# Encoder layer on eight cores: phase-boundary transfers cut into chunks

## The chip, the cores and the metric

The kernel is one program that runs on all 8 cores of one Trainium2 chip. The cores do not speak to each other: each computes 2,048 of the 16,384 tokens, with a halo of 128 tokens on both sides where neighbours are needed. The time is device microseconds of the slowest core. The profile is of one execution, on core 7, the slowest in it.

## What is computed

The reference is one layer of an encoder trunk, on x of 16384 x 2048:

```python
x = layer_norm(ALPHA * x + 0.5 * swiglu(x, ffn1...), ln1)
x = layer_norm(ALPHA * x + hybrid_mixer(x, ...), ln2)
x = layer_norm(ALPHA * x + 0.5 * swiglu(x, ffn2...), ln3)
# swiglu: (silu(x @ w_gate) * (x @ w_up)) @ w_down, with D_FF = 5632
# hybrid_mixer: h = x @ w_in, split into q | k | v | pool channels | gate_a | gate_b
#   y_a = banded attention(q, k, v) @ w_proj_attn        (16 heads, 4 kv heads, |t-s| <= 128)
#   y_b = multiscale pooling(pool channels) @ w_proj_pool
#   (sigmoid(gate_a) * y_a + sigmoid(gate_b) * y_b) @ w_out
```

## The kernel before

Activations are held feature-major: 16 chunks of 128 features on the partitions, tokens along the row. Everything large lies in one on-chip arena. Matmuls run in bf16; weights are f32 in DRAM and are cast by the transfer that loads them.

The work goes through phases, with a token tile each that fits the arena, and every intermediate is written to DRAM and read back by the next phase:

- Phase A, `ffn_phase` for the first SwiGLU, three tiles of 768 tokens: load x (`zf_load`, L420), cast to XB (L432), gate and up projections, down projection in two halves that accumulate into ZF. While the last half runs, `ln_stats` gathers sums. Then `ln_finish` normalizes ZF chunk by chunk: DVE subtracts and multiplies (L372, L380), ACT applies gain and bias in place (L384) and copies the chunk before to bf16 in XB (L387). After all 16 chunks, one store of ZF (L473), one of XB (L476), then the load of the next tile into ZF. `kvp_hook` follows on the same XB: key, value and pooling projections (K, V, P) with 8 weight pieces of `w_in`, and their stores (L510, L522, L534).
- Pooling (L541), two halves of 1,024 tokens.
- Attention (L623), two halves: 4 groups of heads (g) by 8 query blocks (i). The result AT is stored once at the end (L754), then the next stage's weights are prefetched.
- Merge (L771), two halves: projections and gates; MG is filled chunk by chunk (L810) and stored once (L812), then weights are prefetched.
- Output projection (L828), two halves: loads MG (L838) and the residual into ZF (L840), accumulates `w_out` into ZF (L851), `ln_stats`, `ln_finish`, then one store of ZF (L859) and one of the bf16 copy YB (L861), and prefetches.
- Phase C, `ffn_phase` again for the second SwiGLU, tiles of 768, 768 and 512 tokens. It has no bf16 output and no hook.

Order: each engine has its own instruction list, filled in program order. All activations' loads and stores are issued by SP, one after another. All weights are issued by POOL with `load_w` (L291), into a ring of 6 slots (8 in the merge phase), in order: a load waits until the matmuls that used its slot are done. `prefetch_w` issues loads ahead of a boundary. A `P.barrier()` stands at the end of each phase and of each half: every engine waits there for everything issued, all transfers included, prefetched weights too.

The waits are worked out from `Buf` objects. `_waits` adds, for each buffer read, its last write, and for each buffer written, its last write and all its reads:

```python
for b in reads:
    add(b.lastw)
for b in writes:
    add(b.lastw)
    for k, tok in b.reads.items():
        add(tok)
```

The destination in DRAM is such a buffer too: one for the whole of `x1T`, `x2T`, `attnTd`, `mrgTd` and `outT`. A wait on a transfer is put into the list of the engine that issues. In the output projection the four partial sums of `ln_stats` keep 4 of the 8 PSUM banks reserved.

Of the kernel before, what the change touches and what calls it, by code (L numbers as in the profile page):

```python
# [15 lines left out]
DC = 16  # L16
SEQ = 16384
TOWN = SEQ // NCORES
HALO = 128
# [12 lines left out]
C_LN = 0  # L32
# [141 lines left out]
def build_program():  # L174
# [16 lines left out]
    x1T = dt("x1T", [D, TPAD], F32, kind="Internal").ap()  # L191
# [5 lines left out]
    attnTd = dt("attnTd", [D, TOWN], BF16, kind="Internal").ap()  # L197
    mrgTd = dt("mrgTd", [D, TOWN], BF16, kind="Internal").ap()
    x2T = dt("x2T", [D, TOWN], F32, kind="Internal").ap()
    x2bT = dt("x2bT", [D, TOWN], BF16, kind="Internal").ap()  # L200

    def fm(ap2d, c0, nchunk, t0, nt):
        return ap2d[c0 * 128:(c0 + nchunk) * 128, t0:t0 + nt].rearrange("(c p) t -> p c t", p=128)

    ARENA_W = 51200
    with ExitStack() as stack:
# [8 lines left out]
        P = Prog(nc, stack)  # L215
# [87 lines left out]
        def acc(parts, rhs_fn, n_out, extra_reads, U):  # L303
# [3 lines left out]
            for (sa, sb, kc) in parts:  # L307
# [15 lines left out]
             reads=[cst_b], writes=[misc_b])  # L323
        pw_b = Buf("pw")
        P.dma("pool", lambda g: g.dma_start(out=pwsb[:], in_=pwg.rearrange("g (k p) n -> p g k n", p=128)),
              pw_b, writes=[pw_b])
# [24 lines left out]
                     t.matmul(o, onesS[:], r, start=f, stop=la),  # L351
                     reads=[qab, misc_b], writes=[qb[ui][1]], signal=True)

        def ln_finish(st, ZF, zf_b, Tt, units, lncol, YB, yb_b):
            sb, qb = st
            for ui, (u0, U) in enumerate(units):
                m = mean_sb[:, u0:u0 + U]
                r = rstd_sb[:, u0:u0 + U]
                P.op("act", lambda a, o=m, i=sb[ui][0][:, 0:U]: a.activation(o, i, AF.Copy),
                     reads=[sb[ui][1]], writes=[mean_b])  # L360
                P.op("dve", lambda v, o=r, i=m: v.tensor_tensor(o, i, i, ALU.mult),
                     reads=[mean_b], writes=[rstd_b])
                P.op("dve", lambda v, o=r, i=qb[ui][0][:, 0:U]:
                     v.scalar_tensor_tensor(o, i, EPS_P, o, ALU.add, ALU.subtract),
                     reads=[qb[ui][1], rstd_b], writes=[rstd_b])
                P.op("act", lambda a, o=r: a.activation(o, o, AF.Sqrt), reads=[rstd_b], writes=[rstd_b])
                P.op("dve", lambda v, o=r: v.reciprocal(o, o), reads=[rstd_b], writes=[rstd_b])  # L367
            for ap_, b_ in sb + qb:
                reserved.discard(banks.index(b_))
            def e_sub(c):  # L370
                z = ZF[:, c, :]
                P.op("dve", lambda v, z=z: v.tensor_tensor(z, z, mean_sb[:, 0:Tt], ALU.subtract),  # L372
                     reads=[zf_b[c], mean_b], writes=[zf_b[c]])

            e_sub(0)
            for c in range(DC):
                z = ZF[:, c, :]
                if c + 1 < DC:
                    e_sub(c + 1)
                P.op("dve", lambda v, z=z: v.tensor_tensor(z, z, rstd_sb[:, 0:Tt], ALU.mult),  # L380
                     reads=[zf_b[c], rstd_b], writes=[zf_b[c]])
                g = ccol(lncol + c)
                b = ccol(lncol + 16 + c)
                P.op("act", lambda a, z=z, g=g, b=b: a.activation(z, z, AF.Identity, bias=b, scale=g),  # L384
                     reads=[zf_b[c], cst_b], writes=[zf_b[c]])
                if YB is not None and c >= 1:
                    P.op("act", lambda a, o=YB[:, c - 1, :], z=ZF[:, c - 1, :]: a.activation(o, z, AF.Copy),  # L387
                         reads=[zf_b[c - 1]], writes=[yb_b])
            if YB is not None:
                P.op("act", lambda a, o=YB[:, DC - 1, :], z=ZF[:, DC - 1, :]: a.activation(o, z, AF.Copy),  # L390
                     reads=[zf_b[DC - 1]], writes=[yb_b])

        def ffn_phase(tiles, xf_d, xb_d, xb_cast, wg, wu, wd, lncol, outf_d, outb_d, hook):
# [7 lines left out]
            xb_b = Buf("xb")  # L401
            zf_ld = Buf("zfld")
            zf_b = [Buf("zf%d" % c) for c in range(DC)]
            ht_b = [Buf("ht%d" % c) for c in range(22)]
            st_b = Buf("zfst")
# [17 lines left out]
            for ti, (t0, units) in enumerate(tiles):  # L423
                Tt = sum(U for _, U in units)
                XB = xb_view(Tt)
                ZF = ZFf_[:, 0:DC * Tt].rearrange("p (c t) -> p c t", c=DC)
# [3 lines left out]
                if xb_cast:  # L430
                    for c in range(DC):
                        P.op("dve", lambda v, o_=XB[:, c, :], i_=ZF[:, c, :]: v.tensor_copy(o_, i_),  # L432
                             reads=[zf_b[c]], writes=[xb_b])
                elif ti == 0:
                    xb_load(0)
                for g in range(2):
                    for s in range(11):
# [3 lines left out]
                        for nn in range(2):  # L441
                            f = s * 2 + nn
                            for (u0, U) in units:
# [5 lines left out]
                                     reads=[bgb], writes=[tb])  # L449
# [3 lines left out]
                    if g == 1:  # L453
                        if (not xb_cast) and ti + 1 < len(tiles):
                            xb_load(ti + 1)
                        lnst = ln_begin(units)
                    for s in range(8):
# [11 lines left out]
                                ln_stats(lnst, ZF, zf_b, n - 2, Tt, units)  # L469
                ln_stats(lnst, ZF, zf_b, DC - 2, Tt, units)  # L470
                ln_stats(lnst, ZF, zf_b, DC - 1, Tt, units)
                ln_finish(lnst, ZF, zf_b, Tt, units, lncol, XB if outb_d is not None else None, xb_b)
                P.dma("sp", lambda s, i_=ZF, o_=fm(outf_d[0], 0, DC, outf_d[1] + t0, Tt):  # L473
                      s.dma_start(out=o_, in_=i_), st_b, reads=zf_b, writes=[outf_d[2]])
                if outb_d is not None:
                    P.dma("sp", lambda s, i_=XB, o_=fm(outb_d[0], 0, DC, t0, Tt): s.dma_start(out=o_, in_=i_),  # L476
                          xb_b, reads=[xb_b], writes=[outb_d[2]])
# [145 lines left out]
        for h in range(2):  # L623
# [24 lines left out]
                sxg_, o = carve(o, 512, F32)  # L648
                EGs.append((egf_, sxg_, Buf("eg%d" % i), Buf("sxg%d" % i)))
            assert o <= MAIN_W, (o, MAIN_W)  # L650
            x1_b, kt_b, vv_b, at_b = Buf("x1"), Buf("kt"), Buf("vv"), Buf("at")
            P.dma("sp", lambda s, o_=X1, i_=fm(x1bT, 0, DC, HALO + h * 1024, 1024): s.dma_start(out=o_, in_=i_),
                  x1_b, reads=[x1bT_db], writes=[x1_b])
            P.dma("sp", lambda s, o_=KT, i_=fm(kTd, 0, 4, h * 1024, 1280): s.dma_start(out=o_, in_=i_),
# [49 lines left out]
            def o_stage(g, i, pts):  # L704
                bO_ap, bO_b = next_bank()
                for j, (pa, pb, blk) in enumerate(pts):
                    P.op("pe", lambda t, o_=bO_ap, l=VV[:, blk, g * 128:(g + 1) * 128], r=pa, f=(j == 0), la=(j == 2):
                         t.matmul(o_, l, r, start=f, stop=la),  # L708
                         reads=[vv_b, pb], writes=[bO_b], signal=(j == 2))
                bD_ap, bD_b = next_bank()  # L710
                for j, (pa, pb, blk) in enumerate(pts):
                    P.op("pe", lambda t, o_=bD_ap, r=pa, f=(j == 0), la=(j == 2):
                         t.matmul(o_, ones1[:], r, start=f, stop=la),
                         reads=[misc_b, pb], writes=[bD_b], signal=(j == 2))
                dn, dnb = DNs[i % 2]
                P.op("dve", lambda v, o_=dn, i0=bD_ap, i1=EGs[g % 2][1]: v.tensor_tensor(o_, i0, i1, ALU.add),
                     reads=[bD_b, EGs[g % 2][3]], writes=[dnb])
                P.op("act", lambda a, o_=dn: a.activation(o_, o_, AF.Ln), reads=[dnb], writes=[dnb])
                P.op("act", lambda a, o_=dn: a.activation(o_, o_, AF.Exp, scale=-1.0), reads=[dnb], writes=[dnb])
                P.op("dve", lambda v, o_=AT[:, g * 4:(g + 1) * 4, i * 128:(i + 1) * 128],  # L720
                     i0=bO_ap.rearrange("p (h q) -> p h q", h=4), i1=dn.rearrange("p (h q) -> p h q", h=4):
                     v.tensor_tensor(o_, i0, i1, ALU.mult),
                     reads=[bO_b, dnb], writes=[at_b])

            def eg_build(g):
                egf_, sxg_, eg_b, sxg_b = EGs[g % 2]
# [15 lines left out]
            for si, (g, i) in enumerate(seq):  # L742
# [8 lines left out]
                if g < 3 and i < 4:  # L751
                    qpiece(g + 1, 2 * i)
                    qpiece(g + 1, 2 * i + 1)
            P.dma("sp", lambda s, i_=AT, o_=fm(attnTd, 0, DC, h * 1024, 1024): s.dma_start(out=o_, in_=i_),  # L754
                  at_b, reads=[at_b], writes=[attn_db])
            if h == 0:
                for g_ in range(3):
                    for s_ in range(2):
# [12 lines left out]
        for h in range(2):  # L771
# [7 lines left out]
            MGf, o = carve(o, DC * 1024, BF16)  # L779
            MG = MGf.rearrange("p (c t) -> p c t", c=DC)  # L780
            assert o <= MAIN_W
            at_b, mt_b, x1_b, mg_b = Buf("at"), Buf("mt"), Buf("x1"), Buf("mg")
            P.dma("sp", lambda s, o_=AT, i_=fm(attnTd, 0, DC, h * 1024, 1024): s.dma_start(out=o_, in_=i_),
                  at_b, reads=[attn_db], writes=[at_b])
            P.dma("sp", lambda s, o_=MT, i_=fm(mixTd, 0, 8, h * 1024, 1024): s.dma_start(out=o_, in_=i_),
# [3 lines left out]
            for s in range(8):  # L789
# [4 lines left out]
                for nn in range(2):  # L794
                    n = s * 2 + nn
                    for u in range(2):
# [11 lines left out]
                        P.op("dve", lambda v, o_=sb2, i0=byb: v.tensor_tensor(o_, i0, o_, ALU.mult),  # L808
                             reads=[bybb, sbb], writes=[sbb])
                        P.op("dve", lambda v, o_=MG[:, n, us], a_=sa, b_=sb2: v.tensor_tensor(o_, a_, b_, ALU.add),  # L810
                             reads=[sab, sbb], writes=[mg_b])
            P.dma("sp", lambda s_, i_=MG, o_=fm(mrgTd, 0, DC, h * 1024, 1024): s_.dma_start(out=o_, in_=i_),  # L812
                  mg_b, reads=[mg_b], writes=[mrg_db])
            if h == 0:
                for s_ in range(2):
                    prefetch_w(wpa, 0, 16, s_ * 256)
# [8 lines left out]

        x2T_db, x2bT_db = Buf("x2T"), Buf("x2bT")
        ring[0] = slots
        for h in range(2):  # L828
            o = 0
            MGf, o = carve(o, DC * 1024, BF16)  # L830
# [1 line left out]
            ZFf, o = carve(o, DC * 1024, F32)  # L832
            ZF = ZFf.rearrange("p (c t) -> p c t", c=DC)
            assert o <= MAIN_W
            mg_b, zf_ld = Buf("mg"), Buf("zfld")
            YB, yb_b = MG, mg_b
            zf_b = [Buf("zf%d" % c) for c in range(DC)]
            P.dma("sp", lambda s, o_=MG, i_=fm(mrgTd, 0, DC, h * 1024, 1024): s.dma_start(out=o_, in_=i_),  # L838
                  mg_b, reads=[mrg_db], writes=[mg_b])
            P.dma("sp", lambda s, o_=ZF, i_=fm(x1T, 0, DC, HALO + h * 1024, 1024): s.dma_start(out=o_, in_=i_),  # L840
                  zf_ld, reads=[x1T_db], writes=zf_b)
            units = [(0, 512), (512, 512)]
            lnst = ln_begin(units)
            for s in range(8):
                sl = load_w(wout, 0, 16, s * 256)
                for nn in range(2):
# [7 lines left out]
                        ln_stats(lnst, ZF, zf_b, n - 2, 1024, units)  # L854
            ln_stats(lnst, ZF, zf_b, DC - 2, 1024, units)
            ln_stats(lnst, ZF, zf_b, DC - 1, 1024, units)
            ln_finish(lnst, ZF, zf_b, 1024, units, C_LN + 32, YB, yb_b)
            st_b = Buf("zfst")
            P.dma("sp", lambda s, i_=ZF, o_=fm(x2T, 0, DC, h * 1024, 1024): s.dma_start(out=o_, in_=i_),  # L859
                  st_b, reads=zf_b, writes=[x2T_db])  # L860
            P.dma("sp", lambda s, i_=YB, o_=fm(x2bT, 0, DC, h * 1024, 1024): s.dma_start(out=o_, in_=i_),  # L861
                  yb_b, reads=[yb_b], writes=[x2bT_db])
            if h == 0:
# [105 lines left out]
```

How the kernel before makes its waits and increments, by code:

```python
    def replay(self, engname, handle):  # L164
        for waits, fn, inc in self.engs[engname].ops:
            for sem, val in waits:
                handle.wait_ge(sem, val)
            if fn is not None:
                ins = fn(handle)
                if inc is not None:
                    ins.then_inc(inc[0], inc[1])
```

## Time and profile before

| | us |
|---|---|
| median of 2 runs | 7022.39 (7019.82 to 7024.96) |
| the profiled execution | 7022.11 |
| its span (core 7, slowest) | 7020.6 |
| spans of the 8 cores | 6940.3 to 7020.6 |
| PE busy | 5719.6 |
| granted PE clock, mean | 0.910 |

Times in the rows are microseconds from the span's start. The profiled execution is 1.5 us longer than its span. "SPq" marks transfers issued by SP, "L300 POOL" those of weights. The time "to landing" runs from the issue to the completion semaphore.

### The profile page before, as it was taken

The page shows a single profiled execution, that of the slowest core. Times are in us where ns is not written, and L with a number is a line of the kernel's source. Part 1 is how long each engine was busy: PE and PEld are TensorE (multiplying, and loading weights), DVE is VectorE, ACT ScalarE, POOL GpSimd, SP SyncE. Part 2 cuts the span into 40 slices and gives each one's busy share as a digit, 9 for nine tenths or more (in the row PEclk, how much of TensorE's full clock was granted, in tenths as well). Part 3 has the DMA queues.
Part 4 walks back from the last instruction along what each step waited for, and adds up shares of the span by engine and source line. Part 5 has one row for each costly group of instructions (what it writes and reads, how often), then busy time and mean ns, then how long its engine had stood idle before and what let it go on. Part 6 is the DMA issues. An engine that isn't in the chain of part 4 may idle for free.

```text
span 7020.6 us, 83583 instructions; the slowest of 8 cores (6940.3 to 7020.6 us)
## 1 busy us (share of the span) xinstructions
PE 5719.6 (81%) x33856; PEld 3331.1 (47%) x33856; DVE 1212.6 (17%) x1834; ACT 1106.5 (16%) x1785; POOL 880.8 (13%) x729
## 2 busy tenths in 40 slices
PE   7999689996899961656479699537399989998997
PEld 4565455654556540212134244213256556565886
DVE  1111211112111124121211011032111131113112
ACT  0001200012000121343400001132100120002002
POOL 1111001110011103232300000000011111111111
PEclk9999899998999985878789799768699999999998
DMA  9898998989778774232366755744678788868998
GB/s 137 94 110 90 160 116 93 111 90 162 113 91 109 90 132 98 58 50 61 55 113 73 137 63 63 150 123 86 164 94 112 104 138 125 108 91 126 164 142 112
DMA packets 1142409, 756.63 MB, mean 108 GB/s; under 512 B 10128, under 2 KB 1070224, under 8 KB 1142032
## 3 DMA queue, kind: packets, MB, share of 16 engines
q0 software_dynamic: 1050640, 533.24, 65.1%
q1 hardware_dynamic: 91392, 218.03, 10.1%
q8 instruction: 277, 4.54, 0.3%
q14 instruction: 100, 0.82, 0.0%
HBM read 1179.05 MB, written 105.38 MB: 183 GB/s over the span
## 4 chain that ended last, share of the span: by engine, by line
PE 75%; DMA 9%; DVE 5%; another core or an unknown queue 4%; issue 3%; ACT 3%; POOL 1%; SPq 0%; ACTq 0%; DVEq 0%; POOLq 0%
PE ps L314 72%; DMA arena<-ffn_w_up 2%; DVE arena L372 2%; DMA arena<-x1bT 1%; DMA arena<-w_in 1%; DMA x2bT<-arena 1%; ACT arena L694 1%; PE ps L518 1%; DMA arena<-ffn_w_down 1%; DMA arena<-mrgTd 1%; DMA arena<-x2bT 1%; DVE arena L367 1%; DMA arena<-w_out 1%; ACT arena L732 1%
## 5 line engine op out<-in xcount | busy, mean ns | idle before, releaser
L314 PE MATMUL ps<-arena 128*128 128x384 bf16 (+2 forms) x32128 | 5391.4, 331 | 1026.5 <-DMA arena<-x1bT 191.5
L314 PEld LDWEIGHTS ps<-arena 128*128 128x128 bf16 x32128 | 3159.3, 98 | 3240.5 <-issue 1122.3
L448 ACT ACTIVATE arena<-ps 128x384 f32<-128x384 f32 (+1 forms) x528 | 249.5, 474 | 2977.8 <-PE ps L314 2977.8
L451 DVE TENSOR_TENSOR arena<-ps,arena 128x384 bf16<-128x384 f32 (+1 forms) x528 | 282.7, 536 | 2402.4 <-PE ps L314 2386.7
L300 POOL DMA_DIRECT2D arena<-ffn_w_gate x132 | 150.8, 1142 | 2209.6 <-PE ps L314 1961.0
L466 DVE SCALAR_TENSOR_TENSOR arena<-ps,arena 128x384 f32<-128x384 f32 (+1 forms) x384 | 205.7, 536 | 1171.8 <-PE ps L314 925.7
L300 POOL DMA_DIRECT2D arena<-ffn_w_down x192 | 203.2, 1061 | 1372.9 <-PE ps L314 1072.9
L341 ACT ACTIVATE arena<-arena 128x768 bf16<-128x768 f32 (+2 forms) x128 | 111.4, 871 | 942.6 <-DVE arena L466 549.3
L699 POOL TENSOR_TENSOR arena<-arena 128x512 bf16<-128x512 f32 x128 | 188.2, 1491 | 490.5 <-ACT arena L694 404.4
L300 POOL DMA_DIRECT2D arena<-ffn_w_up x132 | 151.4, 1147 | 280.1 <-PE ps L314 232.6
L806 DVE TENSOR_TENSOR arena<-ps,arena 128x512 f32<-128x512 f32 x64 | 44.3, 692 | 646.9 <-ACT arena L804 646.9
L384 ACT ACTIVATE arena<-arena,cstsb 128x768 f32<-128x768 f32 (+2 forms) x128 | 134.8, 1055 | 75.4 <-DVE arena L380 73.2
L708 PE MATMUL ps<-arena 128*128 128x512 bf16 x192 | 65.6, 413 | 95.2 <-POOL arena L699 95.2
L300 POOL DMA_DIRECT2D arena<-w_in x72 | 82.5, 1153 | 384.0 <-PE ps L314 263.7
L804 ACT ACTIVATE arena<-ps 128x512 f32<-128x512 f32 x64 | 38.3, 598 | 583.8 <-PE ps L314 583.8
L699 DVE TENSOR_TENSOR arena<-arena 128x512 bf16<-128x512 f32 x64 | 48.6, 759 | 461.2 <-ACT arena L694 461.2
L380 DVE TENSOR_TENSOR arena<-arena 128x768 f32<-128x768 f32 (+2 forms) x128 | 126.0, 990 | 0.0
L372 DVE TENSOR_TENSOR arena<-arena 128x768 f32<-128x768 f32 (+2 forms) x128 | 125.4, 985 | 0.0
L609 PE MATMUL ps<-arena,pwsb 128*128 128x512 bf16 x64 | 29.6, 617 | 112.1 <-DVE arena L601 112.1
L694 ACT ACTIVATE arena<-ps,cstsb 128x512 f32<-128x512 f32 x192 | 117.3, 684 | 1.7 <-POOL arena L699 1.7
L343 ACT ACTIVATE arena<-arena 128x768 bf16<-128x768 f32 (+2 forms) x128 | 109.3, 854 | 0.0
L851 DVE SCALAR_TENSOR_TENSOR arena<-ps,arena 128x512 f32<-128x512 f32 x64 | 44.1, 692 | 376.0 <-DMA arena<-x1T 195.9
(59 smaller groups left out, 1377.3 us busy)
## 6 DMA issues: line engine op xcount, KB each, us to landing
arena<-ffn_w_gate POOLq DMA_DIRECT2D x132, 1024.0 KB, 12.8
arena<-ffn_w_up POOLq DMA_DIRECT2D x132, 1024.0 KB, 17.1
arena<-ffn_w_down POOLq DMA_DIRECT2D x192, 704.0 KB, 11.5
arena<-w_in POOLq DMA_DIRECT2D x72, 1024.0 KB, 27.0
arena<-xT SPq DMA_DIRECT2D x3, 6144.0 KB, 56.2
x1T<-arena SPq DMA_DIRECT2D x3, 6144.0 KB, 24.8
arena<-x1bT SPq DMA_DIRECT2D x4, 4096.0 KB, 22.8
arena<-w_proj_attn POOLq DMA_DIRECT2D x16, 1024.0 KB, 15.1
```

What stands on the lines that cost most here:

```text
L300: P.dma("pool", lambda g, dst=dst, src=src: g.dma_start(out=dst, in_=src), b, writes=[b])
L314: t.matmul(o, l, r, start=f, stop=la),
L341: P.op("act", lambda a, o=za[:, 0:Tt], i=ZF[:, c, :]: a.activation(o, i, AF.Copy), reads=[zf_b[c]], writes=[zab])
L343: P.op("act", lambda a, o=qa[:, 0:Tt], i=ZF[:, c, :]: a.activation(o, i, AF.Square), reads=[zf_b[c]], writes=[qab])
L372: P.op("dve", lambda v, z=z: v.tensor_tensor(z, z, mean_sb[:, 0:Tt], ALU.subtract), reads=[zf_b[c], mean_b], writes=[zf_b[c]])
L380: P.op("dve", lambda v, z=z: v.tensor_tensor(z, z, rstd_sb[:, 0:Tt], ALU.mult), reads=[zf_b[c], rstd_b], writes=[zf_b[c]])
L384: P.op("act", lambda a, z=z, g=g, b=b: a.activation(z, z, AF.Identity, bias=b, scale=g), reads=[zf_b[c], cst_b], writes=[zf_b[c]])
L448: P.op("act", lambda a, o_=ta[:, 0:U], i_=bg: a.activation(o_, i_, AF.Silu), reads=[bgb], writes=[tb])
L451: v.tensor_tensor(o_, i0, i1, ALU.mult),
L466: v.scalar_tensor_tensor(z, i0, C_FFN, z, ALU.mult, ALU.add),
L694: a.activation(o_, i_, AF.Exp, bias=km, scale=SCALE),
L699: g_.tensor_tensor(o_, i0, i1, ALU.mult),
```

## The change

One large transfer becomes several at seven places. Stores that had to wait for a whole tile are issued for each part as soon as it is final:

- `ln_finish` gets a callback after L384's activation of chunk c; both `ffn_phase` and the output projection use it to store chunk c of ZF (384 KB for 768 tokens, 512 KB for 1,024, 256 KB for 512).
- AT is stored for each group of heads (4 stores of 1 MB), MG for each chunk (16 stores of 256 KB), inside their loops.
- The load of ZF in the output projection is issued as 4 loads of 4 chunks, each with a semaphore of its own.

The number of bytes and the rows of a transfer stay as they are. The destinations in DRAM keep their one buffer each.

```diff
+                if on_chunk is not None:
+                    on_chunk(c)
...
-                ln_finish(lnst, ZF, zf_b, Tt, units, lncol, XB if outb_d is not None else None, xb_b)
-                P.dma("sp", lambda s, i_=ZF, o_=fm(outf_d[0], 0, DC, outf_d[1] + t0, Tt):
-                      s.dma_start(out=o_, in_=i_), st_b, reads=zf_b, writes=[outf_d[2]])
+                def store_chunk(c, ZF=ZF, t0=t0, Tt=Tt):
+                    P.dma("sp", lambda s, i_=ZF[:, c, :],
+                          o_=outf_d[0][c * 128:(c + 1) * 128, outf_d[1] + t0:outf_d[1] + t0 + Tt]:
+                          s.dma_start(out=o_, in_=i_), st_b, reads=[zf_b[c]], writes=[outf_d[2]])
+
+                ln_finish(lnst, ZF, zf_b, Tt, units, lncol, XB if outb_d is not None else None, xb_b,
+                          on_chunk=store_chunk)
...
-                     reads=[bO_b, dnb], writes=[at_b])
+                     reads=[bO_b, dnb], writes=[at_g[g]])
+                if i == 7:
+                    P.dma("sp", lambda s_, i_=AT[:, g * 4:(g + 1) * 4, :], o_=fm(attnTd, g * 4, 4, h * 1024, 1024):
+                          s_.dma_start(out=o_, in_=i_), atst_b, reads=[at_g[g]], writes=[attn_db])
...
-                             reads=[sab, sbb], writes=[mg_b])
-            P.dma("sp", lambda s_, i_=MG, o_=fm(mrgTd, 0, DC, h * 1024, 1024): s_.dma_start(out=o_, in_=i_),
-                  mg_b, reads=[mg_b], writes=[mrg_db])
+                             reads=[sab, sbb], writes=[mg_c[n]])
+                    P.dma("sp", lambda s_, i_=MG[:, n, :], o_=mrgTd[n * 128:(n + 1) * 128, h * 1024:(h + 1) * 1024]:
+                          s_.dma_start(out=o_, in_=i_), mgst_b, reads=[mg_c[n]], writes=[mrg_db])
...
-            P.dma("sp", lambda s, o_=ZF, i_=fm(x1T, 0, DC, HALO + h * 1024, 1024): s.dma_start(out=o_, in_=i_),
-                  zf_ld, reads=[x1T_db], writes=zf_b)
+            for q4 in range(4):
+                P.dma("sp", lambda s, o_=ZF[:, q4 * 4:(q4 + 1) * 4, :], i_=fm(x1T, q4 * 4, 4, HALO + h * 1024, 1024):
+                      s.dma_start(out=o_, in_=i_), zf_ld4[q4], reads=[x1T_db], writes=zf_b[q4 * 4:(q4 + 1) * 4])
...
-            ln_finish(lnst, ZF, zf_b, 1024, units, C_LN + 32, YB, yb_b)
             st_b = Buf("zfst")
-            P.dma("sp", lambda s, i_=ZF, o_=fm(x2T, 0, DC, h * 1024, 1024): s.dma_start(out=o_, in_=i_),
-                  st_b, reads=zf_b, writes=[x2T_db])
+
+            def store_chunk4(c, ZF=ZF, h=h, zf_b=zf_b, st_b=st_b):
+                P.dma("sp", lambda s, i_=ZF[:, c, :], o_=x2T[c * 128:(c + 1) * 128, h * 1024:(h + 1) * 1024]:
+                      s.dma_start(out=o_, in_=i_), st_b, reads=[zf_b[c]], writes=[x2T_db])
+
+            ln_finish(lnst, ZF, zf_b, 1024, units, C_LN + 32, YB, yb_b, on_chunk=store_chunk4)
```

## Rows read from the trace of the kernel before

**Rows 1.** The page, part 1: busy time of the engines.

```profile
PE 5719.6 (81%) x33856; PEld 3331.1 (47%) x33856; DVE 1212.6 (17%) x1834; ACT 1106.5 (16%) x1785; POOL 880.8 (13%) x729
```

**Rows 2.** Chain of waits, whole span, in time: start, length, what.

```profile
835.19 31.20 PE ps L314 x192
...
1733.30 28.94 another core or an unknown queue
...
3106.49 66.38 another core or an unknown queue
...
3951.08 41.52 DMA arena<-w_in
...
4414.04 39.02 DMA arena<-w_out
4453.43 22.78 DMA arena<-mrgTd
...
4678.81 35.23 DMA x2bT<-arena
```

**Rows 3.** Timeline, end of phase A's first tile: start, length, what.

```profile
762.40 1.03 ACT L384 ACTIVATE arena<-arena,cstsb 128x768 f32<-128x768 f32 x1 [5.29 <-DVE arena L380]
...
813.38 2.62 SPq L420 DMA_DIRECT2D arena<-xT  x1
...
888.74 13.33 PE L314 MATMUL ps<-arena 128*128 128x384 bf16 x64 [22.35 <-DMA arena<-w_in]
...
902.18 10.96 DVE L432 CAST arena<-arena 128x768 bf16<-128x768 f32 x16 [66.39 <-PE ps L314]
```

**Rows 4.** Transfers issued from 730 to 930: number, KB, us to landing.

```profile
x1T<-arena SPq DMA_DIRECT2D x1, 6144.0 KB, 23.8
arena<-xT SPq DMA_DIRECT2D x1, 6144.0 KB, 56.2
```

**Rows 5.** Timeline, end of the second tile; landing of L420's loads.

```profile
1629.23 1.03 ACT L384 ACTIVATE arena<-arena,cstsb 128x768 f32<-128x768 f32 x1 [5.29 <-DVE arena L380]
...
1681.18 2.74 SPq L420 DMA_DIRECT2D arena<-xT  x1
...
DMA to landing us min/median/max: 27.6/33.8/62.3
```

**Rows 6.** A lone 3 MB store: in the chain, and in windows (DMA share, GB/s last).

```profile
2618.27 10.39 DMA pTd<-arena
...
2619.00:2620.00 1.00, 0.00 (x0) 0.00 (x0) 0.00 (x0) 0.00 (x0) 0.00 (x0) 1.00 0.85 338
...
2627.00:2628.00 1.00, 0.00 (x0) 0.00 (x0) 0.00 (x0) 0.00 (x0) 0.00 (x0) 0.50 0.33 111
```

**Rows 7.** Window in the attention boundary (DMA share and GB/s last).

```profile
3140.00:3150.00 10.00, 0.00 (x0) 0.00 (x0) 0.00 (x0) 0.00 (x0) 0.00 (x0) 0.50 1.08 106
```

**Rows 8.** Output projection: start of both halves, and the load of x1T.

```profile
4476.35 16.66 PE L314 MATMUL ps<-arena 128*128 128x512 bf16 x64 [65.22 <-DMA arena<-mrgTd]
...
4511.40 9.30 PE L314 MATMUL ps<-arena 128*128 128x512 bf16 x32 [18.39 <-DVE arena L851]
...
4773.97 9.42 PE L314 MATMUL ps<-arena 128*128 128x512 bf16 x32 [20.77 <-DVE arena L851]
...
arena<-x1T SPq DMA_DIRECT2D x1, 8192.0 KB, 56.6
```

**Rows 9.** Timeline, output projection, first chunk finished by L384.

```profile
4641.52 1.24 ACT L384 ACTIVATE arena<-arena,cstsb 128x1024 f32<-128x1024 f32 x1 [6.89 <-DVE arena L380]
```

**Rows 10.** Waits of PE between 6440 and 6960: us, times, longest.

```profile
PE ps L314 <- DMA arena<-ffn_w_down: 14.8, 6, 7.3
```

**Rows 11.** End of the kernel: timeline (L384, L474), and the store's landing.

```profile
6988.75 0.82 ACT L384 ACTIVATE arena<-arena,cstsb 128x512 f32<-128x512 f32 x1 [3.69 <-DVE arena L380]
...
7007.20 0.38 SPq L474 DMA_DIRECT2D outT<-arena  x1
...
outT<-arena SPq DMA_DIRECT2D x1, 4096.0 KB, 12.4
```

More of the change, by code:

```diff
@@ L352, in ln_stats, with ln_finish @@
                      reads=[qab, misc_b], writes=[qb[ui][1]], signal=True)
-        def ln_finish(st, ZF, zf_b, Tt, units, lncol, YB, yb_b):
+        def ln_finish(st, ZF, zf_b, Tt, units, lncol, YB, yb_b, on_chunk=None):
             sb, qb = st
@@ L650, in build_program @@
             assert o <= MAIN_W, (o, MAIN_W)
-            x1_b, kt_b, vv_b, at_b = Buf("x1"), Buf("kt"), Buf("vv"), Buf("at")
+            x1_b, kt_b, vv_b = Buf("x1"), Buf("kt"), Buf("vv")
+            at_g = [Buf("at%d" % g_) for g_ in range(4)]
+            atst_b = Buf("atst")
             P.dma("sp", lambda s, o_=X1, i_=fm(x1bT, 0, DC, HALO + h * 1024, 1024): s.dma_start(out=o_, in_=i_),
@@ L753, in build_program @@
                     qpiece(g + 1, 2 * i + 1)
-            P.dma("sp", lambda s, i_=AT, o_=fm(attnTd, 0, DC, h * 1024, 1024): s.dma_start(out=o_, in_=i_),
-                  at_b, reads=[at_b], writes=[attn_db])
             if h == 0:
@@ L781, in build_program @@
             assert o <= MAIN_W
-            at_b, mt_b, x1_b, mg_b = Buf("at"), Buf("mt"), Buf("x1"), Buf("mg")
+            at_b, mt_b, x1_b = Buf("at"), Buf("mt"), Buf("x1")
+            mg_c = [Buf("mg%d" % c) for c in range(DC)]
+            mgst_b = Buf("mgst")
             P.dma("sp", lambda s, o_=AT, i_=fm(attnTd, 0, DC, h * 1024, 1024): s.dma_start(out=o_, in_=i_),
@@ L827, in build_program @@
         ring[0] = slots
+        zf_ld4 = [Buf("zfld%d" % i) for i in range(4)]
         for h in range(2):
@@ L834, in build_program @@
             assert o <= MAIN_W
-            mg_b, zf_ld = Buf("mg"), Buf("zfld")
+            mg_b = Buf("mg")
             YB, yb_b = MG, mg_b
```

## The prediction

> **What bounds the kernel now.** PE is busy 5719.6 us of 7020.6 [rows 1]; the change touches none of its instructions. What can move is the rest, some 1300 us of idle PE. I read the chain of waits in order of time next: between long runs of L314 it passes through a few boundaries where nothing but transfers runs. The reader is to see there which transfer ends last [rows 2]: a piece of `w_in` at the end of phase A's tiles (shown as an unknown queue, 28.94 us at 1733, and 22.35 us at 888 [rows 3]), prefetched weights after attention and merge, and L861's bf16 store (35.23 us, and the same again in the second half) in the output projection. Then the timelines around each boundary, and last the transfers' own landing times.
>
> **The catch in the change.** Chunk stores name the same DRAM buffer as written. A written buffer adds a wait for its last write, and that is now the store of chunk c-1. So SP issues chunk c only when chunk c-1 has landed: the 16 stores of a tile form a chain, and each pays its whole latency. What a lone transfer pays: the 3 MB store issued at 2618.27 starts to move bytes at about 2619.15 (share 0.85 of that microsecond), stops near 2627.4 and lands at 2628.66 [rows 6]. So 3.15 MB took 8.25 us, 380 GB/s, and 10.39 - 8.25 = 2.1 us are fixed. The last store of the kernel, 4.19 MB in 12.4 us [rows 11], leaves 1.4 at that rate. I take 1.8, and 0.1 for SP to wake and issue. A chunk then takes 1.9 + 1.03 us at 384 KB, 1.9 + 1.38 at 512 KB, 1.9 + 0.69 at 256 KB: 3.0, 3.3, 2.6. L384 makes a chunk ready every 1.74 us in a tile of 768 (first at 763.4, all by 789.6, where the store that lands at 813.4 after 23.8 us was issued [rows 3, 4]), about 2.3 us for 1,024 tokens [rows 2, 9] and 1.2 us for 512 [rows 11]. So in `ln_finish` the store chain, not ACT, sets the pace. Bounds for 384 KB are 2.5 us from below (1.4 us fixed) and 5 us from above for 384 KB, since a contended megabyte costs more: 6 MB took 23.8 us with few weights beside it, while 9 MB (L476's 3 MB and xT's 6) took 56.2 us with them [rows 4], 1.6 times as long for each.
>
> The Trainium skill (DMA: Bandwidth & Descriptors, Anatomy of one DMA) speaks against cutting transfers that wait on each other: a fixed 2.0 us for each, mostly the receipt of the last write, plus bytes at 436 GB/s. By it the chunks take 2.9, 3.2 and 2.6 us, and the sum below would come out 3 to 6 us lower. It is fitted for the other issue path, and no chained small store is in this trace.
>
> **Phase A, tiles 0 and 1.** Chunk 0 is ready at 763.4 [rows 3]. Of the 16 chunks some run beside weights at about 4 us, others alone at 3.0; I take a mean of 3.6. They land by 763.4 + 57.6 = 821.0. Before, the one store landed at 813.4, where L420 is issued [rows 3]. So L476's store and the xT load, which have the SP queue behind it, run 7.6 us later: xT lands at 813.4 + 56.2 + 7.6 = 877.2. But the big store no longer stands in front of the `w_in` pieces between 789 and 813; the last piece, which landed at 888.7 behind more than 15 MB of the SP queue's, now meets less of it in its way and has until 835.19 + 31.20 = 866.4. I take its wait of 22.35 us as gone. P's last 64 matmuls then take 10.4 us instead of 13.33 (192 took 31.20 at full clock [rows 2]), so the cast L432 could start at 902.2 - 22.35 - 2.9 = 876.9. What is late next is xT itself, 877.2: gain 25.0 us. Tile 1: chunk 0 at 1630.3, chain ends 1687.9, 6.7 us after 1681.2; xT lands at 1681.2 + 62.3 + 6.7 = 1750.2 [rows 5]. P would end at 1733.3 + 10.4 = 1743.7; before, the cast began at about 1733.3 + 28.94 + 0.2 + 13.4 = 1775.9. Gain 25.7. Together 50; bounds 57 (xT never late) and 6 (chunks of 5 us: xT lands 22 us later still in both). L476's store and the K, V, P stores move later behind the chain on SP; only L451 of the next tile waits for them and PE has 8 free banks to run ahead. Tile 2 has no next load and no such wait: 0.
>
> **Attention, two halves.** 3 of AT's 4 MB leave the boundary; 3 stores run inside the loop, where no other transfer does. The boundary is bound by transfers together: 6 or 7 weight pieces and the store. 4 MB at 390 GB/s is 10.75 us of engine time, three quarters 8: gain 16 for both. Bounds: 0 if the weights set it alone, 26 if the store slows them by more than its own time. Merge: 15 of 16 chunks of MG leave: 10 us each, 20 for both, on 41.52 and 39.02 us [rows 2]; bounds 0 and 30. A chunk of MG is 112 matmuls of 512 columns, 24 us (384 columns took 31.20 / 192 = 0.1625 us each), so the chain of waits costs nothing there.
>
> **Load of ZF in quarters, two halves.** PE fills its 4 free banks in 16.66 us from 4476.35, then waits 18.39 us for L851, which needs x1T, all of it landing at 4453.8 + 56.6 = 4510.4 [rows 8]. MG landed first, at 4476.2 [rows 2], so the queue serves in order; the 8 MB then take 34.2 us, a quarter 8.6: it lands near 4485, before PE needs a bank at 4493. The later quarters land at 4493, 4502 and 4510, chunks 4, 8 and 12 are due at 4508 and every 31 us after. So 18.4 us go, and the 32 matmuls after it take 6.9 instead of 9.30 us since PE no longer falls to the low clock: 20.8. Second half: 20.77 + 2.5 = 23.3. Take 43; bounds 0 (quarters share the engines and land together) and 46.
>
> **Output projection, stores.** Chunk 0 ready at 4642.8 [rows 9], chunk 15 issued 15 x 3.3 later at 4692.3, its bytes out at 4694.5; L861's store, behind it on SP, needs 10.75 + 0.8 alone: lands near 4706, before 4714.0 (4678.81 + 35.23 [rows 2]). 8 us each, 16 for both. Bounds: 45 (no chain, store issued at 4678.8 lands at 4691.6) and -35 (chunks of 5 us).
>
> **Phase C.** Tile 0 to 1: the store was behind nothing PE waits for: 0; L420's load is issued later but is due only at the first down projection. Tile 1 to 2: the third tile is short of weights, PE waits 14.8 us for down pieces alone [rows 10]; some of the 6 MB store falls into idle engine time before it: 3 us, bounds 0 and 10. End: chunk 0 at 6989.6, 16 x 2.6 = 41.6: ends at 7031.2. Before, one store issued at 7007.2 landed at 7019.6 [rows 11]: a loss of 12, bounds -27 and +10.
>
> **Sum.** 50 + 16 + 20 + 43 + 16 + 3 - 12 = 136 us off the profiled execution's 7022.1, which is the runs' median within 0.3: 6886 us, 1.9% less. About 2% is what a measurement of this kernel can tell from no change, and 2% is 6882, so the forecast stands on that line.
>
> **The rivals.**
> - *No chain.* The stores flow freely, as the change's words say. For: each chunk's own data are ready. Against: the rule of `_waits`. Phase A 56, output projection 45, end +10, phase C 8, the rest as above: 199 off, 6823. Chance 0.07.
> - *Slow chunks, slower than before.* One mechanism: the latency of a chunk in `ln_finish`'s chains. Each microsecond more costs 32 in phase A, 30 in the output projection, 16 at the end, 78 in all; from 1.75 us more (4.75 us for 384 KB) the change loses, at 2.5 us more it is 6886 + 195 = 7081. For: half of phase A's chain runs beside weights. Against: the lone store of rows 6. Beside it, the Trainium skill (DMA: Bandwidth & Descriptors, Latency and other measured facts) gives DRAM access 2 us at high load against 0.2 on average; no small store here shows it. Chance 0.04.
> - *Weights alone set the boundaries.* After attention weights move at 106 GB/s with the store gone and the engines' share at 1.08 [rows 7]; if that pace is not set by the engines, taking stores away gives nothing. Attention, merge and phase C give 0: 6925. Chance 0.15.
> - *xT late in phase A.* The chain or the weights beside it hold the load back by 20 us more than I take: phase A gives 15: 6921. Chance 0.13.
> - *Quarters land together:* 0 instead of 43: 6929. Chance 0.06.
>
> **How the numbers follow.** The forecast has 0.55, with its own range 6850 to 6920. The range asked for 8 in 10 reaches from 6846 to 6955: it takes the three single misses and leaves out no chain, slow chunks and misses in pairs. Faster by over 2%: 0.07 of no chain and a little over half of the forecast's 0.55, 0.36. Slower by over 2%: 0.02, within slow chunks' 0.04. Within 2%: 0.62.
>
> **What would show it.** Right: on SP the chunk stores are spaced by 3 to 4 us and not by ACT's 1.7 or 2.3, each released by the one before; the last `w_in` piece is waited for by nobody, and L432 starts when xT lands; PE starts the output projection without a gap after 64 matmuls; the chain's last pieces are chunk stores and the span ends 24 us after ACT. Wrong: chunks that follow ACT's pace, chunks of 5 us, boundaries after attention and merge as long as before, or a gap at L851 that stays.

## The result, and the profile after

The changed kernel takes 0.9888 of the time of the kernel before (95% interval 0.9871 to 0.9905): about 79 us less, where 136 were forecast (0.981). It lies in the range of 6846 to 6955: 7022.4 x 0.9888 = 6944. In many executions one die or both ran at a lower granted clock (0.78 to 0.89 for 0.91 to 0.92); the times, ratios and stage lengths here are of undisturbed executions and cores alone. The profiled one took 6916.8 us, its slowest core 6915.2 against 7020.6.

Where the time went is read best stage by stage. This table is worked out from the traces of all 8 cores: each stage runs from the issue of its first load (phase A: from L432's cast of a tile to the next; merge: from its load of x1bT, the third) to that of the next stage; each figure is the median of the cores, or the sum of two such medians where a row names two parts.

| stage | before | after | difference | forecast |
|---|---|---|---|---|
| start to the cast of tile 1 | 902.3 | 914.0 | +11.7 | -25 |
| cast of tile 1 to cast of tile 2 | 863.1 | 854.2 | -8.9 | -25.7 |
| cast of tile 2 to pooling | 851.5 | 851.1 | -0.4 | 0 |
| pooling | 193.7 | 186.8 | -6.9 | 0 |
| attention, two halves | 705.6 | 677.6 | -28.0 | -16 |
| merge, two halves | 914.1 | 879.9 | -34.2 | -20 |
| output projection, two halves | 516.5 | 453.0 | -63.5 | -59 |
| phase C | 2041.6 | 2042.0 | +0.4 | +9 |

The median core gained 123 us (6987.9 to 6865.2), the slowest less, since the cores now spread over 124 us instead of 80 and the slowest sets the time. In the medians the forecast failed in one place, phase A's first two tiles: 3 us longer instead of 51 shorter. All the rest together gave more than forecast, 133 us for 86, so that the stages add up to 130 of the forecast 137. The 57 us by which the time fell short of the forecast are then, for the most part, not in this table: the profiled execution is the fastest of the five used here (the others 6938 to 6959), and the slowest core gained less than the median one. In these five the cores spread over 118 to 193 us; those of the kernel before, in nine executions beside the experiments, over 30 to 70. Why the change spreads them was not tried. Tile 2 stores its chunks in a chain too and is as long as before, as forecast. The 7 us of pooling belong to no edit; the same stage differs by as much between executions of one kernel (193.2 and 186.3 in the two of e1's kernel below).

The waits of PE, on the slowest core, core 2 (who waited for what, us, times, longest):

```profile
PE ps L314 <- DMA arena<-x1bT: 185.2, 4, 83.3
PE ps L314 <- DMA arena<-mrgTd: 158.3, 2, 104.6
...
PE ps L314 <- DVE arena L434: 118.3, 3, 46.5
```

L434 is the cast that was L432. The last `w_in` piece, for which PE waited 22.35 us at 888 [rows 3], has gone from this list, as forecast. In its place stands the cast, 118.3 us where L432 had 69.3. The first row is for the most part the boundary before each half of attention, the second that before each half of the output projection. The timeline of the first tile's end shows what it waits for:

```profile
763.32 95.56 SPq L477 DMA_DIRECT2D x1T<-arena  x16
858.98 0.51 SPq L482 DMA_DIRECT2D x1bT<-arena  x1
868.56 2.70 SPq L422 DMA_DIRECT2D arena<-xT  x1
...
910.89 10.50 DVE L434 CAST arena<-arena 128x768 bf16<-128x768 f32 x16 [75.29 <-DMA arena<-xT]
...
921.65 18.67 PE L314 MATMUL ps<-arena 128*128 128x384 bf16 x104 [45.04 <-DVE arena L434]
```

The issues of the 16 chunk stores spread over 95.56 us where ACT makes a chunk ready every 1.74, and the last lands at 868.5; the xT load behind them is issued at 868.56 instead of 813.38 [rows 3] and lands at 910.6. P's last matmul ended at 876.6 (921.65 - 45.04), the 876.9 forecast. So the chain of waits is there and xT is what is late next, but by 34 us. Transfers issued in single moments of this chain (number, KB, us to landing):

```profile
x1T<-arena SPq DMA_DIRECT2D x1, 384.0 KB, 13.9
...
x1T<-arena SPq DMA_DIRECT2D x1, 384.0 KB, 7.9
...
x1T<-arena SPq DMA_DIRECT2D x1, 384.0 KB, 2.3
...
x1T<-arena SPq DMA_DIRECT2D x1, 384.0 KB, 15.3
...
x1T<-arena SPq DMA_DIRECT2D x1, 384.0 KB, 13.4
```

These were issued at 763.3, 777, 790, 808 and 823.6. The slow ones have weights beside them (prefetched ones that land until about 789, and those issued from 804), the fast one has none. Of all 16, those issued while a weight piece was under way took 3.6 to 15.3 us, the others 2.3 to 2.6. What a slow one does with its time stands in the packets. In the 15.3 us of the chunk issued at 808.24 and in the 2.3 us of that issued at 790 the two queues, weights (q0) and SP (q1), had these packets, MB and shares of the 16 engines' time:

```profile
q0 software_dynamic: 2437, 1.24, 93.5%
q1 hardware_dynamic: 144, 0.39, 7.4%
...
q1 hardware_dynamic: 144, 0.39, 43.5%
```

The chunk's own packets need the same in both, some 1.1 us (0.074 x 15.3) and 1.0 (0.435 x 2.3). The rest of the 15.3 us the engines spend on weights: the store is not moved more slowly, it waits among them.

The chains where no weights run are short. Output projection's first half and the kernel's end, SP's timeline:

```profile
4568.82 48.17 SPq L874 DMA_DIRECT2D x2T<-arena  x16
4617.10 0.37 SPq L877 DMA_DIRECT2D x2bT<-arena  x1
```

```profile
6877.87 34.45 SPq L477 DMA_DIRECT2D outT<-arena  x16
```

That is 3.2 us for each of 15 steps of 512 KB (3.0 in the second half), and 2.3 for 256 KB, where 3.3 and 2.6 were forecast. And the start of the output projection (compare with [rows 8]):

```profile
4423.95 1.87 PE L314 MATMUL ps<-arena 128*128 128x512 bf16 x4 [53.68 <-DMA arena<-mrgTd]
4426.04 20.30 PE L314 MATMUL ps<-arena 128*128 128x512 bf16 x90 [0.22 <-issue]
4431.81 0.69 DVE L864 SCALAR_TENSOR_TENSOR arena<-ps,arena 128x512 f32<-128x512 f32 x1 [59.26 <-DMA arena<-x1T]
```

L864 has the residual's first quarter at 4431.8, 7.9 us after MG (8.6 forecast), and PE runs on through the point where it stood for 18.39 us. Last, the pieces of the chain of waits at the boundaries (compare with [rows 2]): 54.33 us for 66.38, 26.33 for 41.52, 26.66 for 39.02, 15.75 for 35.23.

```profile
3096.80 54.33 another core or an unknown queue
...
3926.26 26.33 DMA arena<-w_in
...
4373.19 26.66 DMA arena<-w_out
4400.22 23.59 DMA arena<-mrgTd
...
4617.10 15.75 DMA x2bT<-arena
```

### The profile page after: what moved, and what is told of

Its sections match the earlier page's. It is cut to its first block, busy times and chain, and to the rows that moved or that the text cites. A ratio compares the mean times of both kernels' runs of the same rounds, so it can differ in the third digit from the quotient of the medians.

```text
span 6915.2 us, 83959 instructions; the slowest of 8 cores (6791.6 to 6915.2 us)
## 1 busy us (share of the span) xinstructions
PE 5696.0 (82%) x33728; PEld 3328.0 (48%) x33856; DVE 1211.4 (18%) x1834; ACT 1104.5 (16%) x1785; POOL 880.3 (13%) x729
## 4 chain that ended last, share of the span: by engine, by line
PE 74%; DMA 13%; DVE 4%; ACT 3%; issue 3%; another core or an unknown queue 2%; POOL 1%; SPq 0%; ACTq 0%; DVEq 0%; POOLq 0%
PE ps L314 72%; DMA x1T<-arena 3%; DMA arena<-ffn_w_up 2%; DMA arena<-xT 2%; DMA arena<-x1bT 1%; DMA x2T<-arena 1%; DMA arena<-w_in 1%; ACT arena L702 1%; DVE arena L372 1%; DMA arena<-mrgTd 1%; DMA arena<-x2bT 1%; DVE arena L367 1%; PE ps L351 1%; ACT arena L743 1%
## 5 line engine op out<-in xcount | busy, mean ns | idle before, releaser
L384 ACT ACTIVATE arena<-arena,cstsb 128x768 f32<-128x768 f32 (+2 forms) x128 | 134.5, 1053 | 75.6 <-DVE arena L380 73.3
L300 POOL DMA_DIRECT2D arena<-w_proj_attn x16 | 18.4, 1149 | 697.7 <-PE ps L314 697.7
```

The costliest lines, as they stand in the source:

```text
L300: P.dma("pool", lambda g, dst=dst, src=src: g.dma_start(out=dst, in_=src), b, writes=[b])
```

## The experiments

Two theories of phase A stood against each other: that the chain of waits ate the gain (1), or that stores moved into `ln_finish` only displace the weights there, chained or not (2). Four kernels take the change apart.

**e1_nochain.** The chunk stores of ZF no longer name the DRAM tensor as written. Readers come after a barrier, and the next load into ZF waits for all 16 stores.

```diff
-   ..., st_b, reads=[zf_b[c]], writes=[outf_d[2]])
+   ..., st_b, reads=[zf_b[c]], writes=[])
...
-   ..., st_b, reads=[zf_b[c]], writes=[x2T_db])
+   ..., st_b, reads=[zf_b[c]], writes=[])
```

> The chunk stores of ZF no longer name the DRAM tensor as written, so a store waits only for its own chunk and no longer for the landing of the one before. Theory 1 (the chain of waits is what phase A lost): the 16 stores are issued at L384's pace, the xT load is issued near 815 instead of 869 and lands by 885, the next tile starts some 30 us earlier in both tiles, L861's store is issued 12 us earlier in both halves of the output projection, the end gains 5: about 89 us less than the changed kernel, ratio to the kernel before near 0.976. Theory 2 (stores moved into ln_finish merely compete with the weights there, chained or not): phase A stays as it is, only 29 us go, ratio near 0.985.

Measured: one run, 6853.1, against 7009.2 and 6992.7 for the kernel before on the same chip, 0.979. SP's timeline, and PE's wait at the end of tile 0:

```profile
762.19 26.44 SPq L477 DMA_DIRECT2D x1T<-arena  x16
789.82 0.37 SPq L482 DMA_DIRECT2D x1bT<-arena  x1
811.21 2.84 SPq L422 DMA_DIRECT2D arena<-xT  x1
...
891.34 13.30 PE L314 MATMUL ps<-arena 128*128 128x384 bf16 x64 [19.52 <-DMA arena<-w_in]
```

The stores are issued at ACT's pace, over 26.44 us. But all have landed only at 811.1, where the single store of the kernel before landed at 813.3 (median of the cores 806.8 and 813.6), and the wait for the `w_in` piece is back with 19.52 us. The stage lengths say the same: the cast of tile 1 comes at 896.7, of tile 2 859.4 later (before 902.3 and 863.1). So both theories have a part. The chain made the first tile's end 17 us longer than it had to be (and the second's 5 shorter); but the unchained stores gain 9 us in two tiles (18 in the repetition e7, 892.1 and 854.9), not 50. Against the changed kernel the output projection takes 218.4 and 213.8 for 230.5 and 222.5 (21 us less, 24 expected), and phase C 2024.9 for 2042.0; of these 17 us, where 5 were expected, e7 repeats 5 (2037.0).

**e2_phaseA_whole.** Phase A stores ZF whole; all else as changed.

```diff
+   on_chunk=None if xb_cast else store_chunk)
+   if xb_cast:
+       P.dma("sp", ... fm(outf_d[0], 0, DC, outf_d[1] + t0, Tt) ..., st_b, reads=zf_b, writes=[outf_d[2]])
```

> Phase A's tiles again store ZF in one transfer; all else as changed. Theory 1: the chunks' chain ate nearly all it could give there, stage lengths up to pooling differ by about 5 us; ratio to the kernel before 0.989 to 0.990, and the wait for the last w_in piece (15 to 29 us) is back. Rival (the chunks in phase A carry a good part of the gain, as my prediction's 50 us): 0.995.

Measured: two runs, 6907.1 and 6913.2, ratio 0.987. The theory had said 0.989 to 0.990: without its chunks in phase A the changed kernel is no slower, and perhaps a little faster. The rival's 0.995 is out. The wait for the last `w_in` piece is back as expected, 19.0 to 23.5 us on cores 4 to 7.

**e3_x1T_whole.** The residual's four loads are one again.

```diff
-   for q4 in range(4):
-       P.dma("sp", ... ZF[:, q4 * 4:(q4 + 1) * 4, :] ..., zf_ld4[q4], ...)
+   P.dma("sp", ... ZF ..., zf_ld4[0], reads=[x1T_db], writes=zf_b)
```

> The residual of the output projection is loaded in one transfer again; all else as changed. If the quarters are worth what the stage's timeline says (18 to 20 us of idle PE and 2.5 us of low clock, twice), this is 43 us slower than the changed kernel, ratio to the kernel before near 0.995. Rival (the two halves gained 63 us mainly through the stores): 15 us slower, near 0.991.

Measured: one run, 6959.8, ratio 0.994. The two halves of the output projection take 249.4 and 242.6 us against 230.5 and 222.5: 39 us, for 43 forecast. By subtraction that leaves 24 us to the chunk stores there, for 16 forecast; they have no run of their own.

**e4_AT_MG_whole.** AT and MG are stored whole after their loops.

```diff
-   if i == 7:
-       P.dma("sp", ... AT[:, g * 4:(g + 1) * 4, :] ..., atst_b, reads=[at_g[g]], ...)
+   P.dma("sp", ... AT ..., atst_b, reads=at_g, writes=[attn_db])      # after the loop
...
-   P.dma("sp", ... MG[:, n, :] ..., mgst_b, reads=[mg_c[n]], ...)
+   P.dma("sp", ... MG ..., mgst_b, reads=mg_c, writes=[mrg_db])       # after the loop
```

> AT and MG are stored whole at the end again; all else as changed. The four stages got 62 us shorter in the median of the cores where I had counted 36 (engine time of the bytes moved). Theory 3 (beside weights a store costs more than its engine time, about 1.7 times): 62 us slower than the changed kernel, ratio to the kernel before near 0.998. Rival (engine time only, the rest was chance of the one profile): 36 us slower, near 0.994.

Measured: three runs of 6965.4, 6991.1 and 6992.9, ratio 0.9975. Its three runs differ by 0.4%, so the stages decide: the four halves take 349.0, 355.8, 456.8 and 455.0 us against 337.3, 340.3, 439.3 and 440.6, which is 59 us. The megabytes that stand beside prefetched weights again cost 1.6 times the 36 us of engine time that I had counted. Why they do was not tried.

**e5_quarters_chained.** Phase A stores 4 chained quarters of 1.5 MB.

```diff
+   w = 4 if xb_cast else 1
+   if c % w != w - 1:
+       return
+   c0 = c - w + 1
+   P.dma("sp", ... ZF[:, c0:c0 + w, :] ..., st_b, reads=zf_b[c0:c0 + w], writes=[outf_d[2]])
```

> Phase A's ZF is stored in 4 chained transfers of 1.5 MB instead of 16 of 384 KB; all else as changed. Theory 1 (beside weights a lone transfer pays a latency of some 13 us whatever its size): the chain pays it at most four times, mostly while the next quarter is still being computed; the last quarter lands by 815, xT is issued there instead of near 870, the wait for the last w_in piece comes back (15 to 25 us), the next tile's cast starts near 895. Rival (beside weights these stores get a fixed small rate, 384 KB in 14 us): a quarter takes 50 us beside weights, xT is issued at 860 or later and the cast starts near 915. In time 8 us of 6940, not to be told apart by the clock; the trace decides.

Its executions give no time to compare; the end of tile 0 is read on cores 0, 1, 4 and 5 (granted clock 0.99 up to 760). Core 5, SP and DVE, and the quarters' landing:

```profile
768.34 34.59 SPq L480 DMA_DIRECT2D x1T<-arena  x4
803.02 0.45 SPq L485 DMA_DIRECT2D x1bT<-arena  x1
809.97 2.95 SPq L422 DMA_DIRECT2D arena<-xT  x1
...
886.76 10.96 DVE L434 CAST arena<-arena 128x768 bf16<-128x768 f32 x16 [51.11 <-PE ps L314]
```

```profile
x1T<-arena SPq DMA_DIRECT2D x4, 1536.0 KB, 9.4
```

A quarter lands in a median of 9.4 us (16.9 for the first, 5.7 to 11.4 for the others), with four times the bytes of a chunk that took 3.6 to 15.3 us beside weights in the same place. The xT load is issued at 802.9 to 810.0 on the four cores instead of 852.7 to 887.8, PE waits 8.5 us (21.0 on core 4) for the `w_in` piece again, and the cast starts at 886.8 to 904.1, near the 895 expected. The rival's small fixed rate would have needed some 50 us for a quarter; it is out.

**e10_weights_held.** One POOL memset after each tile of phase A waits until the chain has landed.

```diff
+   if xb_cast:
+       P.op("pool", lambda g: g.memset(scr[:], 0.0), writes=[Buf("scr")] + zf_b)
```

> The changed kernel with one small POOL memset after each tile of phase A that waits until all of the tile's chunk stores have landed, so that POOL issues no weights beside the second part of the chain (those issued before, until 747, still run beside the first chunks); nothing is left out. Theory (a chunk takes 14 us because of the weights beside it, and 2.3 to 3 us alone): after the prefetched weights have landed near 787 every chunk takes about 2.4 us, the chain ends near 818 instead of 853 to 888, and no chunk issued after 790 takes over 4 us. Rival (chunks are slow through something else, the cores' common DRAM traffic or the stores themselves): the chain still ends after 850. The time itself hardly moves, since the last w_in pieces are now issued late and PE waits for them again: 6920 to 6980.

POOL reached the memset before it had issued the hook's first pieces, so all of them were held and the whole chain ran alone. SP's timeline of core 4, and POOL's of core 6:

```profile
766.88 36.02 SPq L478 DMA_DIRECT2D x1T<-arena  x16
...
806.00 1.06 SPq L423 DMA_DIRECT2D arena<-xT  x1
```

```profile
801.29 0.09 POOL L483 MEMSET scr<- 128x1 f32 x1 [99.97 <-DMA x1T<-arena]
801.86 6.85 POOL L301 DMA_DIRECT2D arena<-w_in  x6 [0.47 <-issue]
```

16 chunks in 39 us from the first issue to the last landing; on the eight cores a link takes 2.4 to 2.9 us, and the xT load is issued between 801 and 808, against 853 to 888 in the changed kernel. This shows that the weights beside it make the chain slow: same chunks, same waits, no weights, and 2.4 to 2.9 us instead of 6.6 on average. The time was off what I had expected, 7078.7 for 6920 to 6980, and 1% more than the kernel before on that chip: PE now stood for the held weights, 317.5 us in 8 waits.

**e6_nochain_yb_chunks, e7_nochain_again, e8_nochain_A_whole.** The kernel of e1 once more; with the bf16 copies stored by chunks too, none waiting for the one before; and with phase A's ZF stored whole. The edit of e6:

```diff
+   on_yb(c - 1, yc[c - 1])        # after L387's copy of chunk c-1; a Buf for each chunk
...
-   P.dma("sp", ... YB ..., yb_b, reads=[yb_b], writes=[x2bT_db])
+   P.dma("sp", ... YB[:, c, :] ..., yst_b, reads=[yc], writes=[])
```

> As without the chain, and the bf16 copies (XB in phase A, YB in the output projection) are stored chunk by chunk too, behind the copy of each chunk, with no wait on the one before. In the output projection both stores then run inside ln_finish (12 MB in 36 us, 330 GB/s, under the 360 to 400 of lone stores), and the 14 to 16 us of L877's store after it become 3: 24 us less than without the chain, ratio to the kernel before near 0.975. Rival (12 MB do not fit beside ln_finish, or the 32 transfers of a tile cost SP and the queue more): the last store lands as late as before, no gain.

> The kernel without the chain once more, on the same chip as the others of this call, for an interval: ratio to the kernel before 0.977 to 0.981 if the first look holds, 0.985 or more if it was luck.

> No chain in output projection and phase C, and phase A stores ZF whole as the kernel before. Theory 2 for phase A (a store moved into ln_finish only displaces weights there, so its early start is worth no more than the idle time of the transfer engines, 8.5 us in the first tile): 10 us or less slower than without the chain, stage lengths to pooling as in the kernel before. Theory 1 (without the chain the early start pays as predicted): 40 us slower. On the time alone near 0.980 against 0.985.

| kernel | ratio to before, 95% | output projection, two halves |
|---|---|---|
| e7, no chain | 0.9804 (0.9768 to 0.9841) | 217.8, 212.9 |
| e8, no chain, phase A whole | 0.981 (0.9784 to 0.9837) | 219.1, 215.2 (cores 0 to 3) |
| e6, bf16 copies too | 0.9737 (0.9708 to 0.9766) | 208.4, 207.9 |

e7 confirms e1: the chain costs the changed kernel some 0.8%. e8 answers for phase A: chunk stores there, even unchained, make no difference that the time can tell, and its first two tiles take 1759.6 us for 1747.0 and 1756.1 in the two runs of e1's kernel, so 4 to 13 us where 10 or less were expected and 40 by the other theory. e6 gains 0.7%; 14 us of it are seen in the output projection, where 24 were expected for the whole; the rest lies in no stage that the edit touches.

**e9_inputs_too and e11_inputs_too_again.** e6, and MG loaded in quarters, and x2b ahead of x2 at the start of phase C.

```diff
+   for q4 in range(4):
+       P.dma("sp", ... MG[:, q4 * 4:(q4 + 1) * 4, :] ..., mg_q[q4], reads=[mrg_db], writes=[mg_q[q4]])
...
+   ..., nn, lambda k: [mg_q[k // 4]], U)
...
-   zf_load(0)
-   xb_load(0)
+   xb_load(0)
+   zf_load(0)
```

> As with the bf16 copies in chunks, and two loads that the stages start with: MG of the output projection comes in quarters with a semaphore each (the matmuls over its first 4 chunks wait for the first quarter alone), and phase C loads x2b before x2 (PE needs x2b at once and x2 only at the first down projection). Theory (PE starts when the first needed bytes are there): the 22.7 us before the first matmul of both halves become 8 to 12, but the residual's first quarter now bounds L851's successor, so 5 us each; x2b lands in 16 us instead of 44: 28 us. Together 38 us, ratio to the kernel before near 0.968. Rival (the loads share the engines with prefetched weights, and what lands first makes another late): under 15 us, 0.972 or more.

> The best version so far once more, for an interval. The first look gave one undisturbed run, 6806.3 against 7002.0 (0.972); the stage of phase C was 36 us shorter than with the bf16 copies in chunks, the output projection only 3. If that holds: 0.966 to 0.973.

Measured: 6806.3 against 7002.0, then 6769.3 and 6797.3 against 7007.7 and 7011.5, ratios 0.972 and 0.968. It is the fastest kernel here. Phase C takes 1990.7 and 1994.0 us for 2026.8 in e6, the gain of turning two loads round (28 expected). The quarters of MG gave 0 to 4 us in a half (5 expected): PE starts earlier and then waits for each quarter in turn, eight waits instead of two for nearly the same sum (135.0 us in e6).

```profile
PE ps L314 <- DMA arena<-mrgTd: 125.9, 8, 67.8
```

## Why the prediction was right, and where it was not

**The time.** It came out inside the stated range and on its upper side: 6944 for 6886, outside the 6850 to 6920 that the forecast's own case had. That it did is in part luck. One term missed by 54 us, attention, merge and the stores of the output projection gave 34 more than counted, and the spread of the cores, which the sum does not know, made the slowest core gain less than the median one.

**The catch.** Right. Each chunk store waits for the one before, alone it takes 3.0 to 3.2 us at 512 KB and 2.3 at 256 KB (3.3 and 2.6 forecast), and it sets the pace in `ln_finish`. e1, e6 and e7 show what the change loses by it.

**The step that failed** is "of the 16 chunks some run beside weights at about 4 us, others alone at 3.0; I take a mean of 3.6". The mean in the first tile was 6.6 us (105.2 us for 16), in the second 5.4; beside weights a chunk took 3.6 to 15.3 us, alone 2.3. The prediction gives no working for the 4 us; all it has beside it is the slowing of large transfers, 1.6 times. That factor is one of rate, and a chain of small transfers pays the wait among the weights anew for each: e5 moved four times the bytes in 9.4 us in the same place, and e10 took the weights away and brought every chunk to 2.3 to 3.5. The merge phase shows it once more: its 256 KB chunks of MG land in 2.0 to 2.7 us or, beside a weight piece, in 7.4 to 12.4. So the xT load was issued 55 us later than before instead of 7.6 and, though it took 42.0 us and not 56.2, landed at 910.6 instead of 877.2, and the 25 us of tile 0 turned into a loss of 12. The upper bound, a mean of 5 us, was too low too.

**A second flaw of the same term** would have been hidden by the first: even with a short chain the 50 us were not there. I had let the wait for the `w_in` piece go because the store left its way; e1 and e8 show that the store, early or late, shares the same transfer engines with the same weights. Unchained it landed 7 us earlier (9 in e7), and two tiles gained 9 us (18 in e7). In e1 the two queues fill the engines from the first chunk's issue to the last one's landing (762.2 to 811.1, core 0): packets of SP's take 77% of their time and the weights' 34%, more than all of it as the profile counts packets. I read this as: the bytes between `ln_finish` and the next tile set that boundary, not their order. That the wait was gone in the changed kernel, as forecast, was luck: there the chain had held SP's transfers back, and where the store flows (e1, e7) the wait is back on every core with 2 to 25 us, where it is whole (e2, cores 4 to 7) with 19 to 24.

**Attention and merge.** The mechanism was right and the size off: 62 us in the profile, 59 by e4, where 36 were counted from engine time. The rival that weights alone set these boundaries is out. What makes up the factor of 1.6 stays open.

**Load in quarters.** Right, 39 us by e3 for 43, and the first quarter landed 7.9 us after MG for 8.6. The rival that the quarters land together is out.

**Stores of the output projection.** 24 us for 16, by subtraction; the chunks were a little faster than counted (3.0 to 3.2 us for 3.3), which is worth 6 of these 8.

**Phase C.** +0.4 for +9. At the end of the kernel the span ends 37.4 us after the first chunk is ready, and ended 31 us after it before (7020.6 - 6989.6): a loss of 6 for 12. The other 6 us lie between the tiles, where 3 were forecast, and are within what the stage differs from run to run.

**The rivals.** xT late was the likeliest single one I named beside the weights, and it happened, more strongly than I priced it; attention and merge made up for half of it. No chain did not come about. The mechanism of slow chunks did, but only in phase A, where the chunks cost 54 us of what was forecast, not the 136 that would have been needed to make the kernel slower. (The sum under no chain is 198 us by its own terms, not 199.)

## What to carry to other kernels

Before a large transfer is cut, look at what the pieces wait for: a dependency tracker with one buffer for a whole DRAM tensor makes them a chain, and each piece pays its whole time to landing. Price that time in the place where it will be paid; for 384 KB it was 2.3 us alone and up to 15.3 beside weights here. Where the transfer engines were full across a boundary, in phase A, starting the store earlier gave 4 to 13 us for two tiles (e8). What gave more was to let the consumer start on its first bytes (39 us for the residual, though only 0 to 4 a half for MG), and to load first what is needed first (33 to 36 us in phase C).

## What was not expected of the hardware

- A 384 KB store lands in 2.3 us alone and in up to 15.3 us beside weights on one core (18.2 on another), while 1.5 MB in the same place take a median of 9.4 us. The packets of the slow chunk need some 1.1 us of the engines, those of the fast one 1.0; in between the engines work on weights, 93.5% of the time.
- Keeping 3 to 3.75 MB more of a store next to prefetched weights lengthened a boundary by some 15 us, 1.6 times their engine time.
- The cores, which do not speak to each other, spread over 118 to 193 us with the changed kernel and over 30 to 70 with the kernel before. What spreads them was not tried.
